# Even mixers of a hybrid backbone: recurrence in two token units, gating by block, stages emitted interleaved

## The reference

```
for l in range(4):
    sh1, sc1, g1, sh2, sc2, g2 = ada_mod(cond, w_ada[l], b_ada[l])
    h = x * (1 + sc1) + sh1
    if l % 2 == 0:
        xa, ga, ub, vb = split(h @ w_in_ab[j], 4)
        xc = centred_dwconv(xa)                       # width 4
        for each direction:                           # rg_lru
            a = exp(log_a(sigmoid(wa xc + ba)))       # log_a <= 0
            u = sqrt(1 - a*a) * (sigmoid(wx xc + bx) * xc)
            h_dir = scan(a, u, h0)
        ya = (h_f + h_b) * gelu(ga)
        v  = layer_norm(gelu(vb))
        yb = gelu(ub) * (sgu_ws mixed over chunks of 128 tokens of v + bs)
        mix = concat(ya, yb) @ w_out_ab[j]
    else:
        mix = fourier_mixer(h) @ w_out_c[j]
    x = layer_norm(ALPHA * x + g1 * mix)
    h = x * (1 + sc2) + sh2
    x = layer_norm(ALPHA * x + g2 * (relu(h @ ffn_w1[l])**2 @ ffn_w2[l]))
```

## Time and profile before

| | |
|---|---|
| median of 3 runs | 2273.74 us (2273.14 to 2277.97) |
| profiled execution, time | 2275.71 us |
| its slowest core, span | 2274.0 us (cores 2251.1 to 2274.0) |
| TensorE busy | 1984.6 us (87%) |
| VectorE busy | 1124.7 us (49%) |
| ScalarE busy | 780.7 us (34%) |
| POOL busy | 175.2 us (8%) |
| mean granted TensorE clock, by core | 0.933 to 0.945 |

### The profile page before, as it was taken

The page is one execution under the profiler, slowest core; times in us unless marked ns, Lnnn a source line. Parts: engine busy times, 40 slices in busy tenths (PEclk is TensorE's granted clock), DMA queues, the critical chain, the costliest instruction groups (busy, mean ns, idle before and its releaser), DMA issues.

```text
span 2274.0 us, 26564 instructions; the slowest of 8 cores (2251.1 to 2274.0 us)
## 1 busy us (share of the span) xinstructions
PE 1984.6 (87%) x11152; PEld 952.6 (42%) x11152; DVE 1124.7 (49%) x1635; ACT 780.7 (34%) x1185; POOL 175.2 (8%) x218
## 2 busy tenths in 40 slices
PE   1365989999998899999965688999999888999996
PEld 0132444444444444444421244444444444444443
DVE  0478665431265465322477876553124736542246
ACT  1577343320033443310138834333102444332000
POOL 0000130000001210000000004000000031000000
PEclk9777989999999999999977888999999898999996
DMA  9743225554531036455040211455442301333202
GB/s 196 134 80 53 38 38 88 98 109 85 122 93 42 1 58 128 83 103 104 9 83 0 37 20 25 88 96 110 95 92 111 79 1 38 56 56 56 44 25 100
DMA packets 25039, 163.36 MB, mean 72 GB/s; under 512 B 2876, under 2 KB 3412, under 8 KB 8024
## 3 DMA queue, kind: packets, MB, share of 16 engines
q0 software_dynamic: 18432, 131.34, 32.1%
q1 hardware_dynamic: 6488, 30.33, 3.8%
HBM read 286.63 MB, written 6.34 MB: 129 GB/s over the span
## 4 chain that ended last, share of the span: by engine, by line
PE 70%; DVE 13%; issue 8%; DMA 5%; ACT 3%; another core or an unknown queue 0%; POOL 0%; SPq 0%; DVEq 0%; POOLq 0%; ACTq 0%
PE pb L315 68%; DVE XS L333 4%; DVE BIG L348 2%; DMA XS<-xin 2%; ACT BIG L324 1%; DVE BIG L333 1%; DVE BIG L727 1%; DVE XS L348 1%; DMA RING<-ffn_w 1%; PE pb L318 1%; DMA RING<-w_ada 1%; PE pb L321 1%; DVE RING L348 1%; DMA BIG<-w_out_c 1%; DVE XS L339 1%
## 5 line engine op out<-in xcount | busy, mean ns | idle before, releaser
L315 PE MATMUL pb<-BIG,RING 128*128 128x512 bf16 x3840 | 867.8, 384 | 19.9 <-DMA BIG<-HB 17.2
L315 PE MATMUL pb<-HB,RING 128*128 128x512 bf16 x3648 | 839.7, 392 | 39.9 <-ACT HB L324 15.8
L315 PEld LDWEIGHTS pb<-HB,RING 128*128 128x128 bf16 x3648 | 363.3, 101 | 493.0 <-issue 63.0
L315 PEld LDWEIGHTS pb<-BIG,RING 128*128 128x128 bf16 x3840 | 370.5, 99 | 452.1 <-issue 29.2
L348 DVE SCALAR_TENSOR_TENSOR BIG<-pb,BIG 128x512 bf16<-128x512 f32 x384 | 265.2, 691 | 353.6 <-ACT BIG L324 341.0
L348 DVE SCALAR_TENSOR_TENSOR XS<-pb,MOD,XS 128x512 f32<-128x512 f32 x192 | 143.5, 749 | 586.8 <-PE pb L315 586.8
L324 ACT ACTIVATE BIG<-pb 128x512 bf16<-128x512 f32 (+1 forms) x432 | 256.3, 597 | 505.0 <-PE pb L315 458.1
L324 ACT ACTIVATE HB<-XS 128x512 bf16<-128x512 f32 x192 | 121.0, 630 | 738.2 <-DVE XS L348 737.9
L315 PE MATMUL pb<-BIG 128*128 128x512 bf16 (+4 forms) x568 | 130.9, 373 | 123.2 <-ACT BIG L327 101.8
L333 DVE TENSOR_TENSOR XS<-XS,pb 128x1024 f32<-128x1024 f32 x192 | 231.4, 1215 | 13.6 <-PE pb L321 10.2
L324 ACT ACTIVATE HB<-XS,B2T,G2T 128x512 bf16<-128x512 f32 x168 | 127.0, 803 | 41.3 <-DVE XS L333 41.3
(11 more groups left out here) (76 smaller groups left out, 823.1 us busy)
## 6 DMA issues: line engine op xcount, KB each, us to landing
RING<-ffn_w POOLq DMA_DIRECT2D x64, 1024.0 KB, 8.3
RING<-w_ada POOLq DMA_DIRECT2D x48, 1024.0 KB, 12.4
RING<-w_in_ab POOLq DMA_DIRECT2D x8, 1024.0 KB, 9.4
BIG<-pd SPq DMA_DIRECT2D x4, 2048.0 KB, 10.2
BIG<-w_out_c SPq DMA_DIRECT2D x4, 2048.0 KB, 8.8
XS<-xin SPq DMA_DIRECT2D x8, 768.0 KB, 55.0
yout<-XS SPq DMA_DIRECT2D x12, 512.0 KB, 3.3
RING<-w_out_ab POOLq DMA_DIRECT2D x4, 1024.0 KB, 8.0
```

The source lines that it names most:

```text
L315: P.add("pe", lambda e: e.matmul(out, lhsT=lhsT, rhs=rhs, start=start, stop=stop), reads, writes)
```

## The change

Each even layer is now emitted by `even_region`, as threads (generators), from the last three columns of the preceding w2 to the w1 groups of tiles 0 and 1.
- Every operation carries an estimated duration, and `P.add` keeps an estimated time for each engine and for the end of each operation. `schedule` emits next the thread that is ready first by these estimates, with a penalty for a thread that needs another activation table, and `next_bank` takes the PSUM bank that is estimated free first. The engines' lists and waits work as before.
- The recurrence runs in two token units with buffers of their own: A is blocks 0 and 1 (1024 tokens), B is block 2 (512). Each has a prefix, two chains and a tail thread, one XC buffer instead of two, and one scan per direction and step.
- The minimum over RA, the sum of the directions and the last product of gating are issued on POOL instead of VectorE.
- Gating runs block by block (2, 0, 1), with a square root for each block, and uses the scratch of VG for its temporaries.
- w_in's xa and ga columns are packed so that tile 0 has both for c4 = 0 and 1, tile 1 both for c4 = 2 and 3.
- In layer 0 ada tiles 4 to 9 pass through one slot (slot 1), then w_in tile 1 goes into it; ada tiles 10 and 11 pass through slot 0 once both units have finished the tail of c4 = 1.
- Before layer 2, three columns of w2 are kept instead of four; their groups run in block order 2, 0, 1, and the threads of the mixer start as each block's h is normalised. The four w_in tiles are loaded as the slots come free.
- Output projection and w1 tiles 0 and 1 run in block order 2, 0, 1 as one thread. The two steps of the next layer's ada tiles that stood among those w1 groups come after them. LayerNorm statistics of blocks may share a bank.

The core of the diff:

```diff
+        if dma:
+            self.free[eng] = t + 0.1
+            op.tend = max(t, self.free["dma"]) + cost
+            self.free["dma"] = op.tend
+            op.tend += 2.0
+        else:
+            op.tend = t + cost
+            self.free[eng] = op.tend
+        self.last_end = op.tend
         for b in reads:
...
+    def schedule(ths):
+        now = max(P.free["pe"], P.free["dve"], P.free["act"]) - 2.0
+        while ths:
+            best = None
+            for th in ths:
+                if th.cond is not None:
+                    if not th.cond():
+                        continue
+                    th.cond = None
+                    th.ready = max(th.ready, now)
+                r = th.ready
+                if th.pace:
+                    r = max(r, P.free[th.pace] - 0.3)
+                r += th.bias
+                if th.need is not None and cur["set"] not in th.need:
+                    r += 1.5
+                if best is None or r < best[0]:
+                    best = (r, th)
+            r, th = best
+            now = max(now, min(r, th.ready + 1.0)) if th.pace else max(now, th.ready)
+            P.last_end = th.ready
+            try:
+                y = next(th.gen)
+            except StopIteration:
+                ths.remove(th)
+                th.gen = None
+                continue
+            th.need = None
+            if callable(y):
+                th.cond = y
+            elif isinstance(y, str):
+                th.need = y
+            if not th.pace:
+                th.ready = max(th.ready, P.last_end)
+
...
+        def chain(U, dd):
+            t0, n, bl = UNITS[U]
...
+                yield "E"
+                for i, b in enumerate(bl):
+                    cs_ = slice(i * 512, (i + 1) * 512)
+                    bk, bb = next_bank()
+                    MM(bk[:], GWT[:, dd * 2, c4, :], XCB[:, cs_], True, True, [bGW, bXCB], [bb])
+                    ACT(bk[:], bk[:], AF.Tanh, [bb, bHP], [bb], scale=0.5, bias=hbr)
+                    ACT(RA[:, cs_], bk[:], AF.Exp, [bb, bHP], [bRA], scale=hs_, bias=hs_)
+                    yield
+                PTS(RA, RA, 1.0, ALU.min, [bRA], [bRA])
+                if c4 > 0:
+                    yield has((U, "hsum", c4 - 1))
+                for i, b in enumerate(bl):
+                    cs_ = slice(i * 512, (i + 1) * 512)
+                    bk, bb = next_bank()
+                    MM(bk[:], GWT[:, dd * 2 + 1, c4, :], XCB[:, cs_], True, True, [bGW, bXCB], [bb])
+                    ACT(IG[:, cs_], bk[:], AF.Tanh, [bb, bHP], [bIG], scale=0.5, bias=hbi)
+                    yield
+                fl.add((U, "gates", c4, dd))
+                need = [(U, "gates", c4, 1 - dd)]
+                if c4 > 0:
+                    need.append((U, "tail", c4 - 1))
+                yield has(*need)
+                yield "S"
+                ACT(MU, RA, AF.Square, [bRA], [bMU])
+                ACT(MU, MU, AF.Sqrt, [bMU], [bMU], scale=-0.25, bias=0.25)
+                yield
+                STT(IG, IG, 1.0, XC, ALU.add, ALU.mult, [bIG, bXC], [bIG])
+                fl.add((U, "xcfree", c4, dd))
+                yield
+                TT(MU, MU, IG, ALU.mult, [bMU, bIG], [bMU])
+                yield
+                if U == "A":
+                    if dd == 0:
+                        TS(RAv[:, 1:4, 0:1], RAv[:, 1:4, 0:1], CF[:, 0:1], None, ALU.mult, None, [bRA, bCF], [bRA])
+                    else:
+                        TS(RAv[:, 0:3, 255:256], RAv[:, 0:3, 255:256], CF[:, 0:1], None, ALU.mult, None, [bRA, bCF], [bRA])
+                    init = PT[:, R_H0 + ix:R_H0 + ix + 1]
+                else:
+                    if dd == 0:
+                        MEMZ(RAv[:, 1, 0:1], [], [bRA])
+                    else:
+                        MEMZ(RAv[:, 0, 255:256], [], [bRA])
+                    init = 0.0
+                yield
+                if dd == 0:
+                    SCAN(IG, RA, MU, init, [bRA, bMU, bPT], [bIG])
+                else:
+                    SCAN(IG[:, ::-1], RA[:, ::-1], MU[:, ::-1], init, [bRA, bMU, bPT], [bIG])
+                yield
+                s0_ = 0 if U == "A" else 4
+                VCOPY(ST[:, 16 * s0_ + ix:16 * (s0_ + ns):16], Hv[:, :, 255 if dd == 0 else 0], [bIG], [bST])
+                fl.add((U, "scan", c4, dd))
...
+        def tail(U):
+            t0, n, bl = UNITS[U]
+            for c4 in range(4):
+                yield has((U, "scan", c4, 0), (U, "scan", c4, 1))
+                d = bufs[U]
+                MU = d["MU", 0]
+                bMU = B_[U, "MU", 0]
+                PTT(MU, d["IG", 0], d["IG", 1], ALU.add, [B_[U, "IG", 0], B_[U, "IG", 1]], [bMU])
+                fl.add((U, "hsum", c4))
+                for i, b in enumerate(bl):
+                    yield "G"
+                    bk, bb = next_bank()
+                    group(bk, bb, 1, c4 * 128, b)
+                    ACT(bk[:], bk[:], AF.Gelu_apprx_tanh, [bb], [bb])
+                    TT(ycol(c4, b), MU[:, i * 512:(i + 1) * 512], bk[:], ALU.mult, [bMU, bb], [B_["Y", c4, b]])
+                    yield
+                fl.add((U, "tail", c4))
+
...
+                yield "S"
+                ACT(SDT, MVT[:, :, 1], AF.Sqrt, [bSMV], [bSMV], bias=EPS)
+                P.add("dve", lambda e: e.reciprocal(out=SDT, in_=SDT), [bSMV], [bSMV])
+                for i in range(4):
+                    TS(V[:, i, :], VG[:, i, :], MVT[:, i, 0:1], SDT[:, i:i + 1], ALU.subtract, ALU.mult, [bVG[i], bSMV], [bV[i]])
+                yield has(("w", 2))
...
+                    tmp = VG[:, ti, :]
+                    STT(tmp.rearrange("p (i n) -> p i n", i=4), bk[:].rearrange("p (i n) -> p i n", i=4), gcol,
+                        RT[:, g, :].unsqueeze(1).broadcast_to([128, 4, 128]), ALU.mult, ALU.add, [bb, bPT, bRT], [bVG[ti]])
+                    PTT(ycol(4 + g, b), tmp, VG[:, ui, :], ALU.mult, [bVG[ti], bVG[ui]], [B_["Y", 4 + g, b]])
...
+        def ada_rest():
+            for nb in range(4, 10):
+                ada_load(0, nb, 1)
                 yield
+                ada_mm(0, nb)
                 yield
+            load(1, 1)
+            fl.add(("ada",))
+            yield has(("A", "tail", 1), ("B", "tail", 1))
+            for nb in range(10, 12):
+                ada_load(0, nb, 0)
                 yield
+                ada_mm(0, nb)
                 yield
+            fl.add(("ada2",))
+
+        def loader():
+            yield has(("vdone",))
+            load_wo(0, 2 if w2 is None else res[1])
+
+        def loader0():
+            yield has(("A", "tail", 1), ("B", "tail", 1), ("ada2",), ("wo", 0))
+            load_wo(1, 0 if w2 is None else fs)
+
+        def load_wo(h, i):
+            sl, bs_ = slot_at(i)
+            DMA("pool", sl, w_out_ab[j, h], [], [bs_])
+            pre_wout[l].append((sl.rearrange("p (k n) -> p k n", k=8), bs_))
...
+        def loader1():
+            yield has(("A", "tail", 3), ("B", "tail", 3))
+            load_w1(0, 1 if w2 is None else res[0])
+            yield has(("udone",))
+            load_w1(1, 3 if w2 is None else res[2])
+
+        def out():
+            first = True
+            for b in (2, 0, 1):
+                U = "B" if b == 2 else "A"
+                yield has((U, "tail", 3), ("sgu", b), ("gb", b), ("wo", 0), ("wo", 1), ("ada",))
+                if first:
+                    make_g2b2(0, l, 3, 2 * l)
+                    first = False
+                yield from oproj(l, b, ycol, bY, 2 * l, bg=False)
+                spawn(norm(2 * l, b, 0, "h2"), "ln")
+            for f_ in range(FC):
...
+            for b in (2, 0, 1):
+                yield has(("h2", b))
+                for fq in range(2):
+                    for fl_ in range(4):
+                        w1_group(l, w1pre[l][fq], fq, b, fl_)
+                        yield
+
...
+                fl.add(("gb", b))
+            load(2, 3)
+            spawn(ada_rest(), "ada")
+        else:
+            fl.add(("ada",))
+            fl.add(("ada2",))
+
+            def w2_thread():
+                load(0, fs)
+                blocks = []
+                n_ = 0
+                for y in w2:
+                    if y is None:
+                        n_ += 1
+                        if n_ == 7:
+                            load(1, res[0])
+                        elif n_ == 8:
+                            load(3, res[1])
+                        yield
+                    else:
+                        b = y[1]
+                        if b == 2:
+                            mk2()
+                            load_gwt()
+                            mklru("B")
+                        elif b == 0:
+                            mk0()
+                            load_sgu()
+                            fl.add(("sguw",))
+                        else:
+                            load(2, res[2])
+                            mklru("A")
+                            st["share"] = False
```

(28 more changed lines are left out.)

729 lines of the change are left out of this document (394 added, 335 removed).

## The result

The changed kernel takes 2367.11 us (median of four runs, 2366.12 to 2371.51) against 2273.44 for the kernel before (four runs): a ratio of 1.0421, 95% interval 1.0386 to 1.0456. It is 94 us slower, where 114 us of saving were forecast.

A forecast was written before the change was run, and what follows sets the result against it. TensorE set most of the old time; mixing light and heavy stages was to leave VectorE narrowest in layer 2 and the load chain binding in layer 0. 2275.7 - 54 - 59 = 2162.7, median-corrected to 2160 us; range 2100 to 2230.

The forecast's parts named there:

- The two regions: Re-ordered stretches around the even mixers: layer 2 from 393 to 339 us, layer 0 from 369 to 310.
- the tail: Each region after the large unit's last gate: output groups, normalisation matmuls and w1, TensorE bound, 75 us.
- left out of the sum: Moved ada steps, 0 to 3 us a region, the shared statistics bank and bank choice by time, not counted.
- How full can VectorE be? ... With other work at hand I take 88%.: Layer 2's middle: 178 us of VectorE work at 88% full takes 202 us, plus 8 for POOL.
- the middle: Layer 2 between head and tail, from 33 us to the large unit's last gate at 243; VectorE work 178 us.
- blocking: VectorE time lost to POOL instructions running beside it: 8 us a region, bounds 0 and 48.
- loose: Rival, chance 0.24: all 48 us of POOL block VectorE, 93% full; 21 and 27 us saved, 2226 us.
- the narrowest engine: In layer 2's mixed region VectorE, 265 us before the moves, was said to become narrowest, against TensorE's 257.
- slower: Rival, chance 0.05: the single ada slot starves layer 0; the w_in half must land at 268 to cancel layer 2's 54.
- The recurrence of the small unit starts at 33: Layer 2's head: 21 us for three w2 groups of the last block, then 12 for its normalisation beside w2.
- Some 24 for 1024.: Large-unit recurrence step: 30.7 us for 1536 columns becomes some 24; four from 80 end near 184, the lower bound.
- ada 4 lands at about 79 ... to 144: Layer 0's load chain: ada 4 at 79, five steps of 13 us to 144, last w_in half at 155, binding there.

The follow-up runs named there:

- e6: Changed kernel with the same operations in another, searched emission order (ranks, window, higher table penalty, corrected minimum estimate): 2278.30 us, ratio 1.0032 to the kernel before.
- e3: Changed kernel with only the emission rule's table penalty raised from 1.5 to 6.0: ratio 1.0335 to the kernel before.
- e10: Changed kernel with a searched emission order plus e2 and e4, a repeat run of the same kernel: 2249.79 us, ratio 0.9904 to the kernel before.
- e2: Changed kernel with the nine last w2 groups emitted in pieces of 8 matmuls, addition to XS after the last piece: ratio 1.0398 to the kernel before.
- e4: Changed kernel with layer 0's w_in half for columns 2 and 3 loaded early and gating's ub half last: ratio 1.0397 to the kernel before.
- e8: Changed kernel with the load order of e4 and large unit, small unit and gating run one after the other: 2456.2 us, one run.
- e7b: Kernel of e10 with minimum, sum of directions and gating product back on VectorE and an order searched for that: 2252.13 us, ratio 0.9910 to the kernel before.
- e5: Kernel before with only the minimum, sum of directions and gating's last product moved to POOL: 2355.03 us, ratio 1.0364 to the kernel before.
- e1: Changed kernel with the minimum, sum of directions and gating's last product back on VectorE: 2368.11 us, ratio 1.0426 to the kernel before.
- e9: Kernel before with only the shared bank for LayerNorm statistics: 2262.82 us, ratio 0.9972 to the kernel before.

## Why the prediction was wrong

The two regions were forecast 54 and 59 us shorter; they are 50 and 64 longer. The miss is 104 us in layer 2 (94 before the large unit's last gate, 10 in the tail) and 123 in layer 0 (115 and 8; the last gate is at 350.0). Against it stand 18 us outside the regions that were left out of the sum. 2162.7 + 104 + 123 - 18 is the 2371 to 2372 of the profiled execution.

**The step that failed: "How full can VectorE be? ... With other work at hand I take 88%."** The work of the middle was nearly right: 178 us plus 8 of blocking were forecast, and VectorE has 201 in the changed kernel. The filling was not: 66%. I took engine totals for a bound that mixing would approach. The emission rule takes what is ready first, and the engines work in order, so a piece of output projection, normalisation or gating emitted ahead of a piece of the large unit can delay the one chain that ends last, as the rows of its third and last step show. How much of the miss this is, e6 measures: with the same operations another order takes 89 us back. That is nearly all of the 94 us lost against the kernel before, but less than half of the 207 us between forecast and result. I had this in the rival "loose" as a remark, with a price of 66 us over the forecast where the miss is 207; it needed a price from the diff: the rule gives no rank to the longest chain. How the searched order's gain divides between ranks, window and penalty is open but for the penalty: e3's 20 us, at a higher penalty than e6 has.

**What stays open.** e10, with order, e2 and e4 together, takes 117 us of the changed kernel's time back and is 87 above the forecast in its profile: 65 in layer 0's region, 33 in layer 2's, less 11 outside them. Layer 2's 33 are the longer tail. In layer 0 the large unit's last gate comes at 270.7 where 235 was forecast, with VectorE 71% full, and the tail is 104 us. So the gain of 59 us forecast for layer 0 was seen in no order tried, and which term of its sum is at fault is not shown.

The prediction also calls VectorE the narrowest engine although its own sum gives TensorE 257 us and leaves VectorE 243. For the middle it holds: 201 us busy on VectorE against 182 on TensorE. And "slower", at 0.05, came true as a number only: its mechanism, layer 0 starved by late ada tiles, is worth 9 us in e4.

**"The recurrence of the small unit starts at 33."** With a first prefix of 14 its cast was due at 47; it came at 107. Its normalisation went step by step behind each w2 group's addition. e2 moves the cast by 63 us against that point and the region by 11.5: a real error of the prediction that is worth little while the order is as it is.

**"Some 24 for 1024."** A step alone takes 31 to 33 (e8), as long as for 1536 columns. The step was treated as work that shrinks with its columns. The work did shrink, but the waits from engine to engine did not: in e8 VectorE is idle for 13 to 15 of 33 us and ScalarE for 11 to 12, nearly all of it just before a cast. The split was assumed to cost 5 us of fixed VectorE time; its real price is a second chain of 16 to 18 us a step that has to be hidden. In the changed kernel the large unit's steps in layer 2 took 43 to 58. The lower bound of 184 us for the chain was therefore too low: four steps of 32 and the head of 80 give 208.

**Layer 0: "ada 4 lands at about 79 ... to 144".** The issues came at 89.0 and 218.5. The steps of 13 us became four of 25 to 29 and two of 11, since the loads stood behind the minima and products on POOL's queue, and their matmuls in TensorE's order. I counted POOL's busy time, but not what is queued behind it. Yet the conclusion that this load chain binds was wrong too for the changed kernel: e4 takes the recurrence off it and gains 9 of the 115 us. In e6, whose order is better, TensorE still waits 8.3 us for this tile; what early loading is worth there, no run shows by itself.

**POOL.** The minimum was put at 18 us a layer and at most 30; it is 35. POOL is busy for 106 us in layer 2's region, where 85 were forecast. Blocking was put at 8 us a region, between 0 and 48: VectorE's total of 1116.9 is 28 above the 1089 that follow from the forecast (1124.7 - 46 + 10), 14 a region; e10 against e7b gives 36 of 46, 18 a region, and e5 43, 21 a region. Here the trace bears out the rule that spoke against the move (the Trainium skill, "SBUF — State Buffer", Who interferes with whom: the two engines exclude one another for a whole instruction): the 3.36 us instruction above is 1.28 plus a wait of 2.1, which ends when the POOL sum beside it ends. The move buys nothing in a good order (e7b) or in the changed one (e1), and costs 81 us in the order of before (e5), most of it through loads held back on POOL's queue in layer 0.

**Table loads**: 39 in layer 2's region and 36 in layer 0's, where 40 were forecast, at 1283 ns. The count was right. By e3, 26 fewer give 20 us, less than their 33 us of ScalarE.

**Left out of the sum**: the shared statistics bank, 6 us by e9's ratio. The other 12 of the 18 are open, and no run takes them apart; the place of the ada steps and weight loads is one candidate.

## What to carry to other kernels

Totals per engine bound a mixed stretch from below. How near it comes depends on the order in which a greedy emitter (one that takes whatever is ready first) puts pieces on in-order engines, so find the chain that ends last and ask what gives it precedence. Before a loop is split into smaller units, look at how much of its step is work and how much is hand-over between engines: here only the work shrank. And before work is moved to POOL, price it there, look at what stands behind it on its queue, and count what it takes back from VectorE.

## What the runs showed of the hardware

- A TENSOR_SCALAR minimum in f32 on POOL costs more per column than a two-input operation: 4.08 us for 1536 columns and 1.48 for 512, with VectorE idle beside it, where a sum of two inputs takes 3.42 for 1536 (e5) and 1.27 for 512; on VectorE 0.95 us for 1536.
- VectorE and POOL lengthen each other: 1.28 to 3.36 us on VectorE, 1.26 to 2.04 on POOL for one product of 512 columns in layer 0 of the changed kernel. Of 46 us of VectorE work moved, only 3 (e5), 9 (e10 against e7b) and 18 (changed kernel against e1) showed as less VectorE time. Small instructions suffer most in proportion: a copy of six columns went from 0.16 to 1.79 us in the mean (e5).
- A table load is 1.28 us, and the next activation starts at once behind it; here a switch costs 1.31 us from the end of one activation to the start of the next, not the 2.66 that the prediction quotes. ScalarE of the changed kernel, in order of time:

```profile
1472.93 1.05 ACT L359 ACTIVATE BIG<-BIG 128x1024 f32<-128x1024 f32 x1
1473.99 1.28 ACT L359 ACT_TABLE_LOAD   x1
1475.29 3.09 ACT L359 ACTIVATE BIG<-BIG 128x1024 f32<-128x1024 f32 x3
```
